# Routing of a mixture-of-experts layer by token tile: column groups for the logits, and a first gathering in two halves

## The reference

```python
h = h + group_rms_norm(y, fuse_g[l], N_GROUPS) @ w_out[l]
u = rms_norm(h, norm2_g[l])
...
def moe_ffn(u, router, w_gate, w_up, w_down):      # 256 tokens, 8 experts, TOP_K = 2, D_FF = 2816
    logits = (t @ router).astype(jnp.float32)
    top_v, top_e = lax.top_k(logits, TOP_K)
    top_w = jax.nn.softmax(top_v, axis=-1)
    ...                                            # sort the (token, expert) pairs by expert
    xb = t[row_tok].reshape(n_blocks, MOE_BLOCK, D)
    yb = lax.map(expert_block, (xb, block_e)).reshape(rows, D)     # swiglu with the expert's weights
    out = jnp.zeros_like(t).at[row_tok].add((yb * row_w[:, None]).astype(t.dtype))
```

## Time and profile before

| | |
|---|---|
| time, median of 3 runs | 1201.93 us (1201.83 to 1202.02) |
| span of the profiled execution | 1201.0 us |
| what lies around the span, taken as median less span | 0.9 us |
| PE busy | 1181.9 us (98%) |
| DVE busy | 944.0 us (79%) |
| ACT busy | 836.7 us (70%) |
| POOL busy | 221.3 us (18%) |
| memory traffic | 300 GB/s over the span |

### The profile page before, as it was taken

The page is one execution under the profiler, slowest core; times in us unless marked ns, Lnnn a source line. Parts: engine busy times, 40 slices in busy tenths (PEclk is TensorE's granted clock), DMA queues, the critical chain, the costliest instruction groups (busy, mean ns, idle before and its releaser), DMA issues.

```text
span 1201.0 us, 16975 instructions
## 1 busy us (share of the span) xinstructions
PE 1181.9 (98%) x5860; PEld 985.4 (82%) x5860; DVE 944.0 (79%) x899; ACT 836.7 (70%) x903; POOL 221.3 (18%) x256
## 2 busy tenths in 40 slices
PE   7999999999999999999999999999999999999997
PEld 7988888888888878888888888888888888888885
DVE  4875564455596579999888889889889889898997
ACT  6776644434767767777777777777777778777775
POOL 9976100000597640000000000000000000000000
PEclk9999999999999999999999999999999999999999
DMA  9533975615254399999999999999999999999981
GB/s 309 187 133 130 393 270 175 210 52 178 77 163 158 134 347 394 389 362 388 376 363 384 380 375 367 371 379 366 374 383 367 370 378 363 386 375 359 395 299 54
DMA packets 172933, 357.64 MB, mean 298 GB/s; under 512 B 14555, under 2 KB 45453, under 8 KB 172880
## 3 DMA queue, kind: packets, MB, share of 16 engines
q1 hardware_dynamic: 167600, 344.17, 79.4%
q0 software_dynamic: 5104, 12.51, 3.0%
q10 hardware_dynamic: 176, 0.27, 0.1%
HBM read 351.64 MB, written 8.91 MB: 300 GB/s over the span
## 4 chain that ended last, share of the span: by engine, by line
PE 92%; DVE 5%; ACT 1%; issue 1%; DMA 1%; SPq 0%; DVEq 0%; ACTq 0%
PE bank L1950 16%; PE bank L1952 16%; PE bank L1951 16%; PE bank L1970 7%; PE bank L1968 7%; PE bank L1969 7%; DVE low L1321 2%; PE bank L1994 2%; PE bank L2097 2%; PE bank L2099 2%; PE bank L2098 2%; PE bank L2173 1%; PE bank L1914 1%; PE bank L2175 1%; PE bank L2174 1%; PE bank L1916 1%
## 5 line engine op out<-in xcount | busy, mean ns | idle before, releaser
L1321 DVE TENSOR_TENSOR low<-ring,high 128x2048 fp32r<-128x2048 f32 (+1 forms) x301 | 683.6, 2287 | 127.6 <-ACT high L824 124.2
L824 ACT ACTIVATE high<-ring 128x2048 fp32r<-128x2048 f32 (+1 forms) x326 | 622.5, 1913 | 164.6 <-PE bank L1952 117.5
L1950 PE MATMUL bank<-high,uTh 128*128 128x512 f32 x880 | 348.8, 396 | 1.3 <-DVE low L1321 1.1
L1952 PE MATMUL bank<-high,uTl 128*128 128x512 f32 x880 | 343.3, 390 | 0.0
L1951 PE MATMUL bank<-low,uTh 128*128 128x512 f32 x880 | 342.7, 389 | 0.0
L1950 PEld LDWEIGHTS bank<-high,uTh 128*128 128x128 f32 x880 | 165.2, 188 | 40.1 <-DVE low L1321 5.5
L1952 PEld LDWEIGHTS bank<-high,uTl 128*128 128x128 f32 x880 | 165.2, 188 | 35.4
L1951 PEld LDWEIGHTS bank<-low,uTh 128*128 128x128 f32 x880 | 165.4, 188 | 32.5
L1968 PE MATMUL bank<-high,moe_hTh 128*128 128x512 f32 x320 | 125.3, 391 | 0.0
L1970 PE MATMUL bank<-high,moe_hTl 128*128 128x512 f32 x320 | 124.7, 390 | 0.0
L1969 PE MATMUL bank<-low,moe_hTh 128*128 128x512 f32 x320 | 124.5, 389 | 0.0
(11 more groups left out here) (419 smaller groups left out, 1435.5 us busy)
## 6 DMA issues: line engine op xcount, KB each, us to landing
ring<-in_moe_w_up_dram SPq DMA_DIRECT2D x176, 512.0 KB, 6.7
ring<-in_moe_w_gate_dram SPq DMA_DIRECT2D x176, 512.0 KB, 6.5
ring<-in_moe_w_down_dram SPq DMA_DIRECT2D x176, 512.0 KB, 6.5
ring<-in_w_in_dram SPq DMA_DIRECT2D x36, 512.0 KB, 5.4
ring<-in_ffn_w_up_dram SPq DMA_DIRECT2D x22, 512.0 KB, 6.4
ring<-in_ffn_w_gate_dram SPq DMA_DIRECT2D x22, 512.0 KB, 4.6
ring<-in_ffn_w_down_dram SPq DMA_DIRECT2D x22, 512.0 KB, 4.1
ring<-in_w_out_dram SPq DMA_DIRECT2D x16, 512.0 KB, 3.7
```

The source lines that it names most:

```text
L824: act.activation(high[:, n % SPLIT, 0:width], slot(n)[:, 0:width], ACT.Copy).then_inc(s["high_ready"], 1)
L1321: dve.tensor_tensor(low[:, n % SPLIT, 0:width], slot(n)[:, 0:width], high[:, n % SPLIT, 0:width].bitcast(F32), ALU.subtract).then_inc(s["l ...
L1950: pe.matmul(o, ah, bh, start=(kd == 0), stop=False)
L1952: last = pe.matmul(o, al, bh, start=False, stop=(kd == KD - 1))
```

## The change

Five things change.

1. **Logits.** The router's 8 columns are put into a matrix of 32 columns per block, zeros behind them (`router_wide`). The eight products of a token tile are spread over four column groups of the PE array, each of which writes its own 32 partitions of one bank; two products per group are accumulated. The copy to `logitsT` is then 128 x 128, and a product with `gather_id`, a 128 x 8 matrix with four ones in each column, adds the four groups and transposes in one step (`logits_sum`).
2. **By token tile.** Ranks (`ranks(t)`), selection (`select_first(t)`) and the gathering of expert 0's tokens (`first_tokens(t, groups)`) are done for tile 0 while tile 1 is still on its way; the four banks are accumulated over both tiles.
3. **Second tile in halves.** The transposes of the first half of tile 1 and their copy stand ahead of the last six `w_out` matmuls; ACT copies both halves of tile 1, takes the sum of squares in halves (`square_half`, `halves_rstd`).
4. **Filler.** The `spin` matmuls are gone.
5. **Smaller.** The conversion of the indices to float (L1666) is gone, one of the two `xl` copies moves to ACT, the split of one weight piece by ACT moves behind the `unh` of tile 1 and the next one behind the copies of the gathered tokens, and the table load of ACT moves behind that. The scaling of the router moves from the mixers of layer 2 to DVE's stream right ahead of the routing.

```diff
@@ -352,7 +353,7 @@
         NORM_BANKS = (0, 1, 4, 7)
         Z_BANK = {"b": 0, "a": 5, "mq": 5, "mk": 0, "gqk": 4}
         PAIR_BANKS = {"l": (2, 1), "rg": (6, 5), "vo": (0, 3)}
-        ROUTE_BANKS, LOGITS_BANKS, LOGITT_BANKS = ((0, 1), (4, 2)), (0, 1), (3, 6)
+        ROUTE_BANKS, LOGITS_BANK, TOKEN_BANKS, OVER_BANK, FIRST_BANKS = ((0, 1), (4, 2)), 0, (3, 4), 2, (5, 6, 1, 7)
         FUSE_ORDER = (1, 3, 0, 2)
         FUSE_DONE = ("y_a", "y_c", "y_m", "y_g")
         FUSE_BANKS = (5, 4, 0, 0)
@@ -1169,10 +1170,23 @@
                     act.preload_act_table(ACT.Silu)
                     act.wait_ge(s["rstd_ready"], 4)
                     ffn(DENSE0, None, 0, TT, DENSE_TILES, scale=rstd, start=3)
-            def u32_out(t):
-                act.wait_ge(s["norm_tr"], steps_before(5) + 2 * t + 1)
-                act.activation(u32[:, 0:4, t * P:(t + 1) * P], bank[ROUTE_BANKS[t][0]][:, :].rearrange("p (k n) -> p k n", k=4),
-                               ACT.Copy).then_inc(s["u32_act"], 1)
+            def u32_out(t, half):
+                act.wait_ge(s["norm_tr"], steps_before(5) + 2 * t + half + 1)
+                act.activation(u32[:, 4 * half:4 * half + 4, t * P:(t + 1) * P],
+                               bank[ROUTE_BANKS[t][half]][:, :].rearrange("p (k n) -> p k n", k=4), ACT.Copy).then_inc(s["u32_act"], 1)
+
+            def square_half(t, half):
+                act.wait_ge(s["h_ready"], 8 + 2 * t + half + 1)
+                at = slice(half * 512, (half + 1) * 512)
+                chain.done(act.activation(unl[:, t, at], h[:, t, at], ACT.Square, accum_out=ss[:, t, half:half + 1]))
+
+            def halves_rstd(t):
+                chain.wait()
+                chain.done(act.activation(ss[:, t, 1:2], ss[:, t, 1:2], ACT.Copy, scale=1.0 / D, bias=EPS))
+                chain.wait()
+                chain.done(act.activation(lnv[:, t, 0:1], ss[:, t, 0:1], ACT.Ln, bias=ss[:, t, 1:2], scale=1.0 / D))
+                chain.wait()
+                act.activation(rstd[:, t, 0:1], lnv[:, t, 0:1], ACT.Exp, scale=-0.5).then_inc(s["rstd_ready"], 1)
             def rows_high(t):
                 act.wait_ge(s["hg_ready"], 2 * t + 2)
@@ -1185,14 +1199,23 @@
             act.activation(ones_r[:, :], ones[:, 0:P], ACT.Copy).then_inc(s["route_consts"], 1)
             tile_rstd(0, 2, unl)
-            u32_out(0)
+            u32_out(0, 0)
             rows_high(0)
+            u32_out(1, 0)
+            square_half(1, 0)
+            u32_out(1, 1)
+            square_half(1, 1)
+            halves_rstd(1)
+            rows_high(1)
             split_high(MOE0 + 1)
-            u32_out(1)
-            tile_rstd(1, 2, unl)
-            rows_high(1)
+
+            for i in range(2):
+                act.wait_ge(s["first_T"], i + 1)
+                act.activation(xh[:, 4 * i:4 * i + 4, :], bank[FIRST_BANKS[i]][:, :].rearrange("p (k n) -> p k n", k=4),
+                               ACT.Copy).then_inc(s["first_xh"], 1)
+            act.wait_ge(s["first_T"], 4)
+            act.activation(xl[:, 4:8, :], bank[FIRST_BANKS[3]][:, :].rearrange("p (k n) -> p k n", k=4), ACT.Copy).then_inc(s["first_xh"], 1)
             split_high(MOE0 + 2)
-
             act.wait_ge(s["over_ready"], 1)
             for t in range(TT):
@@ -1426,9 +1445,8 @@
                 chain.done(dve.memset(vaug[:, :, :, DH:DH + 1], 1.0))
                 if l:
-                    dve.wait_ge(s["router_in"], 16)
-                    dve.tensor_tensor(router[:, :, :], router[:, :, :], bc(cols[:, 0, NORM2 + KD:NORM2 + 2 * KD].unsqueeze(2), [P, KD, E]),
-                                      ALU.mult).then_inc(s["router_ready"], 1)
+                    dve.tensor_reduce(gather_id[:, :], ident[:, :].rearrange("p (g e) -> p e g", g=4)[:, 0:E, :], AX_X,
+                                      ALU.add).then_inc(s["router_ready"], 1)
                 if l == 0:
                     split_in("l1")
                 if l:
@@ -1653,20 +1671,18 @@
             def logits_out(t):
                 dve.wait_ge(s["logit_mm"], t + 1)
-                dve.tensor_copy(logitsT[:, t, :], bank[LOGITS_BANKS[t]][0:E, 0:P]).then_inc(s["lt_ready"], 1)
+                dve.tensor_copy(logitsT[:, t, :], bank[LOGITS_BANK][:, 0:P]).then_inc(s["lt_ready"], 1)
             def route(t):
                 dve.wait_ge(s["logit_ready"], t + 1)
-                lg = bank[LOGITT_BANKS[t]][:, 0:E]
+                lg = bank[TOKEN_BANKS[t]][:, 0:E]
                 chain.done(dve.max(top8[:, t, :], lg))
                 chain.wait()
                 chain.done(dve.max_index(idx8[:, t, :], top8[:, t, :], lg))
                 chain.wait()
-                chain.done(dve.tensor_copy(idf[:, t, :], idx8[:, t, :]))
-                chain.wait()
                 chain.done(dve.tensor_tensor(oh[:, t, :, :], bc(iota[:, 0:E].unsqueeze(1), [P, 2, E]),
-                                             bc(idf[:, t, 0:2].unsqueeze(2), [P, 2, E]), ALU.is_equal))
+                                             bc(idx8[:, t, 0:2].unsqueeze(2), [P, 2, E]), ALU.is_equal))
                 chain.wait()
                 dve.tensor_tensor(routed[:, t, :], oh[:, t, 0, :], oh[:, t, 1, :], ALU.add).then_inc(s["routed_ready"], 1)
@@ -1675,29 +1691,35 @@
                 dve.scalar_tensor_tensor(out=unl[:, t, :], in0=un[:, t, :], scalar=rstd[:, t, 0:1],
                                          in1=unh[:, t, :].bitcast(F32), op0=ALU.mult, op1=ALU.subtract).then_inc(s["unl_ready"], 1)
+            def select_first(t):
+
+                dve.wait_ge(s["rank_ready"], t + 1)
+                chain.done(dve.scalar_tensor_tensor(out=rank1[:, t, :], in0=bank[TOKEN_BANKS[t]][:, E:2 * E], scalar=1.0,
+                                                    in1=routed[:, t, :].bitcast(F32), op0=ALU.add, op1=ALU.mult))
+                chain.wait()
+                dve.tensor_scalar(sel[:, t, :], iota[:, :], rank1[:, t, 0:1], -1.0, ALU.subtract, ALU.is_equal).then_inc(s["sel_ready"], 1)
+
+            dve.wait_ge(s["router_in"], 16)
+            chain.done(dve.memset(router_wide[:, :, :], 0.0))
+            chain.wait()
+            dve.tensor_tensor(router_wide[:, :, 0:E], router[:, :, :], bc(cols[:, 0, NORM2 + KD:NORM2 + 2 * KD].unsqueeze(2), [P, KD, E]),
+                              ALU.mult).then_inc(s["router_ready"], 1)
             u32_out(0)
-            rows_low(0)
             add_half(1, 0, OUT_BANKS[2], "out_half", 3)
             logits_out(0)
+            rows_low(0)
             add_half(1, 1, OUT_BANKS[3], "piece_used", MOE0)
-            u32_out(1)
             route(0)
+            select_first(0)
             logits_out(1)
             route(1)
+            select_first(1)
+            rows_low(1)
             chain.done(dve.tensor_tensor(gap[:, :], top8[:, :, 1], top8[:, :, 0], ALU.subtract))
-
-            dve.wait_ge(s["rank_ready"], 1)
-            chain.done(dve.scalar_tensor_tensor(out=rank1[:, :, :], in0=bank[2][:, 0:TT * E].rearrange("p (t e) -> p t e", t=TT), scalar=1.0,
-                                                in1=routed[:, :, :].bitcast(F32), op0=ALU.add, op1=ALU.mult))
-            chain.wait()
             chain.done(dve.tensor_scalar(keys[:, :, 0:E], rank1[:, :, :], -1.0, None, ALU.add))
             chain.wait()
-            for t in range(TT):
-                last = dve.tensor_scalar(sel[:, t, :], iota[:, :], keys[:, t, 0:1], None, ALU.is_equal)
-            last.then_inc(s["sel_ready"], 1)
-            dve.wait_ge(s["rank_ready"], 2)
-            dve.tensor_scalar(over[:, :], bank[4][:, 0:E], float(P), None, ALU.is_gt).then_inc(s["over_ready"], 1)
-            rows_low(1)
+            dve.wait_ge(s["rank_ready"], 3)
+            dve.tensor_scalar(over[:, :], bank[OVER_BANK][:, 0:E], float(P), None, ALU.is_gt).then_inc(s["over_ready"], 1)
             def route_weights():
@@ -2362,83 +2383,91 @@
...
+                    def route_transposes(t, i):
+                        b = ROUTE_BANKS[t][i]
+                        pe.wait_ge(s["h_ready"], 8 + 2 * t + i + 1)
+                        if (t, i) == (0, 1):
+                            claim(b, "u32_dve", 1)
+                        else:
+                            claim(b, "u32_act", t + i + 1)
+                        for k in range(4):
+                            last = pe.transpose(bank[b][:, k * P:(k + 1) * P], h[:, t, (4 * i + k) * P:(4 * i + k + 1) * P], ident[:, :])
+                        last.then_inc(s["norm_tr"], 1)
+
+                    def logits(t, half):
+
+                        if half == 0:
+                            claim(LOGITS_BANK, "lt_ready", t + 1)
+                            pe.wait_ge(s["u32_act"], t + 1)
+                        elif t == 0:
+                            pe.wait_ge(s["u32_dve"], 1)
+                        else:
+                            pe.wait_ge(s["u32_act"], 3)
+                        for g in range(4):
+                            k = 4 * half + g
```

(100 more changed lines are left out.)

39 lines of the change are left out of this document (8 added, 31 removed).

## The result

| | before | with the change |
|---|---|---|
| time, median of 21 runs | 1202.02 us | 1204.14 us |
| ratio to the kernel before | 1 | 1.0013 (95% interval 1.0007 to 1.0019) |
| forecast | | 1198.4 us, 1197.6 to 1200.6 |

The account below looks back on a forecast made before the run. The prediction took a PE-ACT-DVE hand-over, then DVE from its first weight split, to bound the stretch before the experts. A 3.8 us gain less 0.3 for hand-overs gave 1201.9 - 3.5 = 1198.4 us, range 1197.6 to 1200.6.

Parts of the forecast that it names:

- what bounds the stretch: Before the experts, a hand-over among PE, ACT and DVE sets the pace; after 435.59 the chain runs on DVE.
- the logits: On PE, a tile's 8 products in column groups were to take 0.7 us instead of 1.85.
- the copy to `logitsT`: DVE's copy of tile 1's logits was taken as 0.27 us as before, though now with 128 partitions.
- the router ahead of the routing: Router scaling on DVE before the routing, taken as 0.6 us, hidden in 1.24 us; at the upper end costing 0.2.
- the weights: Rival, 7%: PE's start outruns the weight loads of the first experts; 3.0 of 3.5 us could return, 1201.4 us.
- the chain then runs on DVE from the first split: DVE's first weight split was to start at 432.3 instead of 436.20, PE's fourth piece at 441.1 instead of 444.89.
- the prediction's own sign of being wrong: It would be wrong if the granted clock read under 1.00 between 420 and 440 us.
- Without it 0.87: `routed` of tile 0 at 426.1: Tile 0's decision on DVE, without the index conversion, was to take 0.87 us instead of 1.24.
- `unl` of tile 0 runs 422.9 to 424.2 and is just clear of it: DVE's low part of tile 0 was to end before DVE's addition of tile 1's second half at 424.55.
- `sel` of tile 1: Tile 1's selection on DVE was to be complete at 429.7 instead of 431.69, 2.0 us earlier.
- The rival with the falling clock: Rival, 7%: the clock falls in the routing stretch, 5.5 us of PE work runs at half rate, 1203.9 us.
- The longest gap I count is shorter than the one that did nothing: Argument against a clock fall: PE's idle gaps of some 0.4 us against 1.09 us at 12.90, where clock stayed 1.00.

Follow-up runs that it names:

- e6_port_fill: e5_port with seven filler matmuls of 512 columns where PE still waits; 1197.92 us, ratio 0.9969 to the kernel before.
- e9_dense_fill: The changed kernel with 15 filler matmuls, nine in PE's two long waits and six among the gathering; 1200.05 us, ratio 0.9984 to the kernel before.
- e7_serial_logits: The changed kernel with nine fillers in PE's two long waits and the logits in one column group; 1203.29 us, ratio 1.0011 to the kernel before.
- e5_port: The changed kernel, DVE comparing logits in PSUM and GpSimd starting tile 1 after tile 0's `unl`, no fillers; 1199.84 us, ratio 0.9986 to the kernel before.
- e10_port_late3: e6_port_fill with only the last three of its seven fillers, those among the second tile's gathering; 1200.30 us, ratio 0.9988 to the kernel before.
- e2_pool_late: The changed kernel with GpSimd's scaling of tile 0 held until both tiles' low parts are out; 1202.12 us, ratio 1.0008 to the kernel before.
- e4_before_columns: The kernel before with only the logits in column groups, old order and old fillers; 1206.23 us, ratio 1.0025 to the kernel before.
- e8_before_columns_fill: e4_before_columns with five more fillers behind each tile's logits; 1202.03 us, ratio 1.0004 to the kernel before.

## Why the prediction was wrong

I was right on what bounds the stretch, on the logits (0.64 us measured, 0.7 taken), on the copy to `logitsT` (0.29, 0.27 taken), the router ahead of the routing (0.27 + 0.52 measured, hidden), and on the weights, which were not late. That the chain then runs on DVE from the first split holds in e6_port_fill, where PE starts on the fourth piece 19.7 us after the first logits (19.5 by the prediction). In the trace with the change it does not: there the chain is PE's own work at half rate. Two steps failed, and the prediction's own sign of being wrong, a granted clock under 1.00 between 420 and 440 us, came true.

*"Without it 0.87: `routed` of tile 0 at 426.1", and "`unl` of tile 0 runs 422.9 to 424.2 and is just clear of it".* I moved DVE's operations on the clock and took their durations from rows in which GpSimd happened to be quiet. On the clock of the prediction `routed` came at 427.9, 1.8 late, and `sel` of tile 1 at 431.75 instead of 429.7. Nearly all of the 1.8 lies in the steps from `MAX8` to `routed`: 0.87 us by the prediction, 2.54 measured (424.32 to 426.86), because both small tables stood beside GpSimd. The longest stall, 1.04 us of `unl`, costs little. In the new order the addition of tile 1's first half comes before `unl`; it is what releases GpSimd's product, so the two start within 0.04 us of each other. But behind `unl` DVE would have waited for PE anyway, as it does in e6_port_fill for 0.73 us. The trace of the kernel before could have warned me, in the timelines of DVE and GpSimd: the conversion that takes 0.34 us for tile 1 took 0.64 for tile 0, and ended 1.15 us after GpSimd's scaling had begun.

```profile
427.63 0.64 DVE L1666 CAST idf<-idx 128x8 f32<-128x8 uint32 x1
```

```profile
427.12 2.86 POOL L772 TENSOR_SCALAR un<-un,rstd 128x1024 f32<-128x1024 f32 x1
```

The Trainium skill, "SBUF — State Buffer", Who interferes with whom, states the rule I did not look up: DVE and GpSimd share a port pair, held exclusively for a whole instruction, and a DVE operation with two SBUF inputs takes part in it against a GpSimd operation that reads SBUF. The trace agrees for GpSimd's two-input products, about: `oh` ends with one, and `unl` loses 1.04 us beside one of 1.28. For GpSimd's scaling it agrees in part: `routed` ended 1.14 us after the scaling began, and the scaling went on to 428.60. In the kernel before, tile 0's `oh` and `routed`, with two SBUF inputs each, started 1.2 and 1.4 us into the scaling and took 0.17 us each. The measurement decides: beside this operation DVE stood only in its first 1.1 us.

Cost, in time: e9_dense_fill less e6_port_fill, 2.1 us. The traces divide it, as an estimate. Counted from the first logits, `MAX8` of tile 0 comes 0.2 us later with the stalls (3.76 against 3.53), which is what `unl` costs, and from there to `routed` it takes 2.54 instead of 0.69. Of these 1.85, 0.17 is the index search, since tile 1's decision, which meets no stall, takes 0.86 (428.64 to 429.50); 1.7 are the two small tables.

*The rival with the falling clock, 7%.* "The longest gap I count is shorter than the one that did nothing" compared one gap with one gap. e7_serial_logits fell after 9.4 us with 0.04 us of gaps. What the kernel before had in that place was eight fillers and 3.7 us of logits one product after the other; the change removed the fillers and cut the logits to 1.3. Cost: 4.1 us by e9_dense_fill, in a kernel with the stalls. Without them it is 1.9 (e5_port less e6_port_fill), so the two costs do not simply add: either way from the changed kernel to e6_port_fill is 6.2 us. That the rival's time, 1203.9, lies near the 1204.1 measured is luck: it had 5.5 us for the fall and nothing for the stalls.

The rest of the account closes. e6_port_fill has the changed order with neither of the two, 1197.9, where I had 1198.4 (without the index search it is no longer quite the kernel that I forecast); with the stalls 1200.05; with the fall too 1204.1. I lacked one more thing, which the mechanism does not depend on: the trace before was of an execution 1 us later than most.

What stays open: the shares of `unl`, the tables and the index search in the 2.1 us are read from traces and were not run apart, and e9_dense_fill has eight fillers more than e6_port_fill; and what makes the clock stay in six of twelve runs of the very same e10_port_late3 and not in the others I cannot tell from these runs.

## What to carry to other kernels

When a change moves an operation of DVE or GpSimd, write both engines' rows side by side on the new clock and mark each pair in which DVE has two SBUF inputs, and small conversions from SBUF to SBUF, which stood here too; a duration from another place holds only without such a neighbour. Then ask which of them DVE would have spent waiting anyway: here the longest stall cost least. Filler matmuls are part of a kernel's time budget: before they are removed, and before PE's dense work is made shorter, look at what else keeps PE at 2.4 GHz there, over the whole stretch, waits and short products together. A mean granted clock of 0.994 instead of 0.998 in 1200 us was some 4 us (the two groups of e10_port_late3).

## What the runs showed of the hardware

- The granted clock can fall while PE's busy time is complete: 9.36 of 9.40 us busy, then 0.52 (e7_serial_logits). It can stay up while PE is less busy: 6.47 of 6.90 us at 1.00 (e9_dense_fill).
- Eight full float32 products of 32 columns in four column groups take 0.64 us; the eight products of 8 columns before took 1.85 one after the other. Inserted alone, they made the kernel slower, by 4.5 us in the median and 3.0 in the mean (e4_before_columns); with the time filled again, no different (e8_before_columns_fill).
- A DVE operation of 8 columns took 1.05 us beside GpSimd's scaling (the changed kernel) and 0.17 without it (e2_pool_late). A conversion of 8 columns, with one SBUF input, took 1.03 us at the start of the scaling and 0.18 near its end (e4_before_columns).
- Comparisons that read the logits from PSUM ran in 0.22 to 0.23 us beside a GpSimd product of two SBUF inputs (e6_port_fill).
